# Two-layer hybrid trunk on one core: four stages of the mixer moved between attention units, and one PSUM bank left out of the rotation for a while

## The chip, the cores and the metric

The kernel runs on one core of a Trainium2 chip, in one launch, for 256 tokens of width 1024, all in float32. The metric is the device time in microseconds (us); the median of three runs before the change is 1275.85 us (1275.85 to 1276.56).

## The reference

Each of two layers does x += W_out(concat[attention(h), conv(h), retention(h)]) with h = RMSNorm(x), and then x += FFN(RMSNorm(x)): a dense SwiGLU in layer 0, a top-2-of-8 expert SwiGLU in layer 1. A last RMSNorm follows. The mixers read column groups of one projection:

```python
proj = h @ w_in
o_a = nsa_mixer(q, k_c, v_c, k_s, v_s, k_w, v_w, gl, cmp_pe, cmp_w1, cmp_w2)
o_b = conformer_conv(conv_in, conv_w, conv_b, conv_ln_g, conv_ln_b, conv_pw)
o_c = retention(rq, rk, rv, rg, ret_gn)
```

- Attention has 8 heads of 64 in 2 key groups and three branches. With 256 tokens all 4 blocks of 64 are selected and the window of 512 covers everything, so the selected branch and the window branch are both causal softmax attention, with their own keys and values. The compressed branch attends over 15 blocks; its keys and values come from `silu(flat @ w1) @ w2`, once for keys and once for values (the two "compression halves").
- Retention has 4 heads: scores q·k times a decay, then the product with v, a normalisation over each head and a gate: `o = intra + cross`, `mu`, `var`, `silu(gate) * o`.
- The convolution is depthwise with 31 taps, then a LayerNorm over channels, SiLU and a pointwise product.

## The kernel before

Every engine (TensorE, ScalarE, VectorE) walks the same static list `MIXER[l]` of stages for layer l, and takes from each stage its own part. An engine runs its parts strictly in that order; nothing overtakes. The list is the opening (`OPEN`, `HEAD`: projections, convolution taps, rotary, first scores), then 12 attention units, then `TAIL`. A unit k is a piece of one branch: 4 heads by 128 tokens or 2 heads by 128 tokens with 256 keys. Unit k is the stages

`probT k` (transpose of unit k's probabilities, copied by ScalarE), `AHEAD[k]`, `score k+2` (the scores of the unit after next: TensorE, then VectorE's row maximum, then ScalarE's exponentials), `BESIDE[k]`, `pv k` (product with the values: TensorE, then VectorE's scaling).

`BESIDE[k]` holds stages of the other mixers put into that unit. Those that the change touches:

- `rets 0`, `rets 1`: retention's scores. TensorE writes two banks each, VectorE multiplies by the decay (line 1778) into `rp0`, `rp1`.
- `convT`: TensorE transposes the convolution's output; `cnorm 0` is VectorE's mean and variance of it (lines 1805 to 1811).
- `reto`: retention's product, 12 matrix products on TensorE (each is two records in the trace, as every float32 product is), one copy by ScalarE (line 1266). It waits for all of `rets`.
- `hid 0`, `hid 1`: the first products of the two compression halves, 16 matrix products each with 32 weight columns (`128*32` in the trace), one copy by ScalarE (line 1311). They need the weights W1K and W1VN, which SyncE's queue loads.
- `retnorm 0`: VectorE's statistics of `reto` (lines 1784 to 1789); `croot`: ScalarE's inverse root for `cnorm`.

In the trace, line 661 is every matrix product and line 664 every transpose of TensorE. Line 1705 is a unit's row maximum, 1707 its negative, 1298 the exponentials, 1308 the copy of the transposed probabilities, 1712, 1716 and 1719 the scaling of `pv`. Line 1687 is VectorE's 16 additions that read the bank of `kcv` (the compressed branch's raw keys and values) into `blocks`.

PSUM has 8 banks. `GROUP` gives every stage that writes PSUM its bank, by counting round from bank 2 in the order of the list. TensorE's `begin` waits until the last user of that bank has been read (`bank_free`). The bank of a score stage is freed by ScalarE when the exponentials of that unit are done. From `out 0` on, only banks 0 to 3 rotate.

Of the kernel before, what the change touches and what calls it, by code (L numbers as in the profile page):

```python
# [76 lines left out]
def conv(a, b):  # L77
# [12 lines left out]

AHEAD = {6: [("convB", 0), ("hidT", 0), ("hidT", 1), ("rsilu", 0), ("rroot", 0)], 8: [("retcat", 0)]}

BESIDE = {0: [("rets", 0)], 1: [("rets", 1)], 2: [("convT", 0)],
          3: [("reto", 0), ("hid", 0), ("cnorm", 0)], 4: [("croot", 0), ("hid", 1), ("retnorm", 0)], 5: [("cnorm", 1)],
          6: [("retnorm", 1)], 7: [("cmpkv", 0), ("conv_pw", 0)],
          8: [("cscore", 0), ("out", 0)], 9: [("out", 1)],
          10: [("cprobT", 0), ("out", 2), ("cpv", 0), ("cpv", 1)],
# [6 lines left out]
                           for z in [("probT", k)] + AHEAD.get(k, []) + [("score", k + 2)] * (k + 2 < len(UNITS)) +  # L104
                           BESIDE[k] + [("pv", k)]] + TAIL for l in range(DEPTH)]
EARLIER = (("stat", 0), ("nT", 0), ("stat", 1), ("split", 0))
# [7 lines left out]
OUT_BANK = (4, 5, 6, 7)  # L114
FIXED = {("out", r): OUT_BANK[r] for r in range(4)}
FIXED.update({("xT", 0): 2, ("xT", 1): 3, ("xT", 2): 2, ("xT", 3): 3})
NARROW = [MIXER[l].index(("out", 0)) for l in range(DEPTH)]
BANKS = 8
# [16 lines left out]
GROUP = {}  # L135
_used = [0] * BANKS
for _l in range(DEPTH):
    _n = 2
    for _at, (_stage, _k) in enumerate(MIXER[_l]):
        for _j in range(STATED.get((_stage, _k), PSUM_GROUPS.get(_stage, 0))):  # L140
            if (_stage, _k) in FIXED:
                _b = FIXED[_stage, _k]
            else:
                _b = _n % (BANKS if _at < NARROW[_l] else OUT_BANK[0])
                _n += 1
            _used[_b] += 1
            GROUP[(_l, _stage, _k, _j)] = (_b, _used[_b])

# [2131 lines left out]
```

## Time and profile before

| | us |
|---|---|
| median of three runs | 1275.85 |
| the profiled execution's own time | 1274.48 |
| its span (first to last instruction) | 1272.5 |
| TensorE, matrix products busy in the span | 1253.3 (98%) |
| VectorE busy | 996.7 (78%) |
| ScalarE busy | 857.3 (67%) |

The span is one execution on the chip. It is 1.98 us shorter than the time of that execution, which also holds what lies around the instructions. A busy TensorE means that records of matrix products follow each other; their ends are modelled. The granted TensorE clock is 0.997 of full speed over the span. The mixer's units of layer 0 lie from 81 to 152 us, those of layer 1 from 416 to 487 us. The rest of the span is the projections, the dense FFN and the experts.

### The profile page before, as it was taken

To read this page: it belongs to the slowest core of one execution; us is meant where nothing else is said; L and a number is where in the kernel's file an instruction comes from. 1 tells how busy PE (TensorE), PEld (TensorE's weight loads), DVE (VectorE), ACT (ScalarE), POOL (GpSimd) and SP (SyncE) were. 2 spreads that over 40 slices of the span, in tenths; PEclk is the share of its full clock that TensorE was granted. 3 is DMA by queue.
4 is the path that set the end of the run, shared out by engine and by line. 5 is a ranking of instruction groups with operands and counts; after the bars stand their busy time and mean duration, and the time that the engine had idled before them with its cause. 6 is when DMAs were issued, how large, how long until landed. Compare 5 with 4: busy or idle time off the path is not lost.

```text
span 1272.5 us, 16272 instructions
## 1 busy us (share of the span) xinstructions
PE 1253.3 (98%) x6317; PEld 1015.6 (80%) x6317; DVE 996.7 (78%) x1110; ACT 857.3 (67%) x1225; POOL 31.4 (2%) x21
## 2 busy tenths in 40 slices
PE   9999999999999999999999999999999999999997
PEld 8797588888779866788888888888888888888885
DVE  4786465454569646998999989889889889889997
ACT  5435364444451544978878888878878878878885
POOL 0000000000000000010000000000000000000300
PEclk9999999999999999999999999999999999999998
DMA  9433194442521336899999999999999999999981
GB/s 366 169 143 133 67 387 174 175 190 103 198 100 71 143 132 271 335 404 373 391 371 371 389 380 375 388 369 377 396 369 379 389 374 357 396 373 353 416 368 39
DMA packets 38625, 367.62 MB, mean 289 GB/s; under 512 B 4112, under 2 KB 7312, under 8 KB 11152
## 3 DMA queue, kind: packets, MB, share of 16 engines
q1 hardware_dynamic: 35808, 356.56, 71.2%
q0 software_dynamic: 1440, 5.24, 1.1%
q10 hardware_dynamic: 1296, 4.72, 0.9%
q8 instruction: 53, 0.87, 0.3%
q14 instruction: 28, 0.23, 0.1%
HBM read 360.73 MB, written 5.77 MB: 288 GB/s over the span
## 4 chain that ended last, share of the span: by engine, by line
PE 92%; DVE 4%; ACT 2%; DMA 1%; issue 1%; SPq 0%; DVEq 0%; ACTq 0%
PE ps L661 88%; PE ps L664 3%; DMA ring<-mix_in 1%; ACT arena L1298 1%; DVE blocks L1687 1%; DVE wlU L1869 1%; DVE arena L1705 0%; DVE wlD L1876 0%; ACT arena L1308 0%; ACT L1290 0%; ACT L1345 0%; DVE arena L1778 0%; DVE xn L2112 0%; DVE hTl L1991 0%; DVE x L1833 0%
## 5 line engine op out<-in xcount | busy, mean ns | idle before, releaser
L1869 DVE TENSOR_TENSOR wlU<-ring,whU 128x2048 fp32r<-128x2048 f32 x196 | 448.9, 2290 | 57.7 <-ACT whU L1390 53.1
L1390 ACT ACTIVATE whU<-ring 128x1024 fp32r<-128x1024 f32 x396 | 417.6, 1060 | 60.8 <-PE ps L661 53.2
L661 PE MATMUL ps<-whU,hTh 128*128 128x512 f32 x880 | 352.7, 401 | 0.8 <-DVE wlU L1869 0.8
L661 PE MATMUL ps<-whU,hTl 128*128 128x512 f32 x880 | 345.0, 392 | 0.0
L661 PE MATMUL ps<-wlU,hTh 128*128 128x512 f32 x880 | 342.9, 390 | 0.0
L1876 DVE TENSOR_TENSOR wlD<-ring,whD 128x2048 fp32r<-128x2048 f32 x97 | 222.2, 2290 | 39.2 <-ACT whD L1402 39.0
L1402 ACT ACTIVATE whD<-ring 128x1024 fp32r<-128x1024 f32 x194 | 205.2, 1066 | 59.0 <-PE ps L661 52.8
L661 PEld LDWEIGHTS ps<-whU,hTl 128*128 128x128 f32 x880 | 165.1, 188 | 36.0
L661 PEld LDWEIGHTS ps<-wlU,hTh 128*128 128x128 f32 x880 | 166.1, 189 | 32.4
L661 PEld LDWEIGHTS ps<-whU,hTh 128*128 128x128 f32 x880 | 165.3, 188 | 32.7 <-DVE wlU L1869 1.0
L661 PE MATMUL ps<-whD,gTh 128*128 128x512 f32 x428 | 168.6, 394 | 0.5 <-DVE gTl L1894 0.5
L661 PE MATMUL ps<-whD,gTl 128*128 128x512 f32 x428 | 167.3, 391 | 0.0
L661 PE MATMUL ps<-wlD,gTh 128*128 128x512 f32 x428 | 166.6, 389 | 0.0
L661 PEld LDWEIGHTS ps<-whD,gTh 128*128 128x128 f32 x428 | 80.4, 188 | 19.7 <-DVE wlD L1876 3.6
L661 PEld LDWEIGHTS ps<-whD,gTl 128*128 128x128 f32 x428 | 80.3, 188 | 16.9
L661 PEld LDWEIGHTS ps<-wlD,gTh 128*128 128x128 f32 x428 | 80.7, 189 | 16.4
L1416 ACT ACTIVATE gTh<-ps 128x256 fp32r<-128x256 f32 x107 | 40.3, 386 | 54.6 <-PE ps L664 54.6
L661 PEld LDWEIGHTS ps<-arena 128*128 128x128 f32 (+1 forms) x472 | 56.6, 190 | 14.5 <-issue 12.7
L661 PE MATMUL ps<-arena 128*128 128x64 f32 (+6 forms) x472 | 65.2, 297 | 2.3 <-ACT arena L1308 2.3
L1894 DVE TENSOR_TENSOR gTl<-ps,gTh 128x256 fp32r<-128x256 f32 x107 | 44.3, 422 | 27.5 <-ACT gTh L1416 27.5
L664 PE MATMUL ps<-cst,arena 128*128 128x128 f32 x376 | 63.3, 273 | 1.2 <-DVE arena L1815 1.1
L664 PEld LDWEIGHTS ps<-cst,arena 128*128 128x128 f32 x376 | 48.2, 143 | 17.2 <-issue 3.6
(232 smaller groups left out, 1224.2 us busy)
## 6 DMA issues: line engine op xcount, KB each, us to landing
ring<-moe_in SPq DMA_DIRECT2D x88, 2048.0 KB, 8.5
ring<-moe_in SPq DMA_DIRECT2D x88, 1024.0 KB, 8.6
ring<-ffn_in SPq DMA_DIRECT2D x11, 2048.0 KB, 7.5
ring<-mix_in SPq DMA_DIRECT2D x5, 3072.0 KB, 11.0
ring<-ffn_in SPq DMA_DIRECT2D x11, 1024.0 KB, 7.2
ring<-mix_in SPq DMA_DIRECT2D x4, 2048.0 KB, 10.3
ring<-mix_in SPq DMA_DIRECT2D x2, 2176.0 KB, 8.3
ring<-mix_in SPq DMA_DIRECT2D x2, 2112.0 KB, 8.1
```

The lines of the kernel that those rows point to most:

```text
L661: return nc.tensor.matmul(o, lhsT, rhs, start=first, stop=last, skip_group_check=True)
L664: return nc.tensor.transpose(o, a, ident)
L1298: last = A(prob[:, k % 3, c * keys:(c + 1) * keys], bank(l, stage, k)[:, c * keys:(c + 1) * keys], ACT.Exp, bias=nmax[:, k, c:c + 1], scal ...
L1390: A(whU[:, p, :], ring[:, f.slot(J), p * PIECE:(p + 1) * PIECE], ACT.Copy).then_inc(s_hi, 1)
L1402: A(wh_down(f, J, c), ring[:, f.slot(J), (UP + c) * PIECE:(UP + c + 1) * PIECE], ACT.Copy)\
L1416: A(g_high(f, J, i), ps[:, up_bank(f, J, i), 0:FC].rearrange("p (c t) -> p c t", c=DOWN), ACT.Copy)\
L1687: last = V.tensor_tensor(blocks[lo:lo + HD, v, hi, :, g, 0:NBLK], src[g * HD:(g + 1) * HD, v, :, hi:hi + NBLK, r], spread(pe_[lo:lo + HD, ...
L1869: V.tensor_tensor(wlU[:, w, :], raw, whU[:, w, :].bitcast(F32), ALU.subtract).then_inc(s_lo, 1)
L1876: V.tensor_tensor(wl_down(f, J), raw, high.bitcast(F32), ALU.subtract).then_inc(s_lo, 1)
L1894: V.tensor_tensor(g_low(f, J, i), ps[:, up_bank(f, J, i), 0:FC].rearrange("p (c t) -> p c t", c=DOWN), g_high(f, J, i).bitcast(F32), ALU.s ...
```

## The change

The new order of `BESIDE` puts `rets 1` into unit 0 beside `rets 0`, `convT` into unit 1, `cnorm 0` and `reto` into unit 2, and `croot`, `hid 0` and `hid 1` into unit 3. All engines follow it. In the bank rotation, the bank of `kcv` is skipped from `kcv` until `pv 0`. All later banks of the units shift with it.

```diff
-BESIDE = {0: [("rets", 0)], 1: [("rets", 1)], 2: [("convT", 0)],
-          3: [("reto", 0), ("hid", 0), ("cnorm", 0)], 4: [("croot", 0), ("hid", 1), ("retnorm", 0)], 5: [("cnorm", 1)],
+BESIDE = {0: [("rets", 0), ("rets", 1)], 1: [("convT", 0)], 2: [("cnorm", 0), ("reto", 0)],
+          3: [("croot", 0), ("hid", 0), ("hid", 1)], 4: [("retnorm", 0)], 5: [("cnorm", 1)],
...
 for _l in range(DEPTH):
-    _n = 2
+    _n, _held = 2, None
     for _at, (_stage, _k) in enumerate(MIXER[_l]):
+        if (_stage, _k) == ("pv", 0):
+            _held = None
         for _j in range(STATED.get((_stage, _k), PSUM_GROUPS.get(_stage, 0))):
             if (_stage, _k) in FIXED:
                 _b = FIXED[_stage, _k]
             else:
-                _b = _n % (BANKS if _at < NARROW[_l] else OUT_BANK[0])
+                _wide = BANKS if _at < NARROW[_l] else OUT_BANK[0]
+                _n += _n % _wide == _held
+                _b = _n % _wide
                 _n += 1
+            if _stage == "kcv":
+                _held = _b
             _used[_b] += 1
             GROUP[(_l, _stage, _k, _j)] = (_b, _used[_b])
```

The banks of the first stages, in the order of each version (the same in both layers), with the last user of the bank behind the arrow:

```
before: kcv 3, score0 4, score1 5, probT0 6, score2 7, rets0 0 and 1, pv0 2, probT1 3<-kcv, score3 4<-score0,
        rets1 5<-score1 and 6<-probT0, pv1 7<-score2, probT2 0<-rets0
after:  kcv 3, score0 4, score1 5, probT0 6, score2 7, rets0 0 and 1, rets1 2 and 4<-score0, pv0 5<-score1,
        probT1 6<-probT0, score3 7<-score2, convT 0<-rets0, pv1 1<-rets0, probT2 2<-rets1, score4 3<-kcv
```

## Rows read from the trace of the kernel before

**Rows 1.** The page: busy time and share of each engine over the span.
```profile
PE 1253.3 (98%) x6317; PEld 1015.6 (80%) x6317; DVE 996.7 (78%) x1110; ACT 857.3 (67%) x1225; POOL 31.4 (2%) x21
```

**Rows 2.** Chain of waits that ended last, layer 0's units: start, duration, what.
```profile
88.76 1.52 ACT arena L1298 x8
...
92.65 6.50 PE ps L661 x69
...
100.73 0.70 DVE arena L1705
...
106.22 1.03 ACT arena L1298 x4
...
114.84 1.08 PE ps L661 x8
```

**Rows 3.** Timeline, TensorE's weight loads, units 0 to 4: start, duration, what, idle before.
```profile
84.00 0.97 PEld L661 LDWEIGHTS ps<-arena 128*128 128x128 f32 x8 [0.33 <-issue]
85.12 0.42 PEld L664 LDWEIGHTS ps<-cst,arena 128*128 128x128 f32 x4 [0.15 <-DVE blocks L1687]
85.51 0.10 PEld L661 LDWEIGHTS ps<-causalb,identb 128*128 128x128 bf16 x1
...
86.81 0.52 PEld L661 LDWEIGHTS ps<-arena 64*128 64x128 f32 x8
...
89.17 0.10 PEld L661 LDWEIGHTS ps<-causalb,identb 128*128 128x128 bf16 x1
...
90.04 0.57 PEld L664 LDWEIGHTS ps<-cst,arena 128*128 128x128 f32 x4
91.09 0.97 PEld L661 LDWEIGHTS ps<-arena 128*128 128x128 f32 x8 [0.48 <-issue]
91.93 0.48 PEld L664 LDWEIGHTS ps<-cst,arena 128*128 128x128 f32 x4
92.38 0.10 PEld L661 LDWEIGHTS ps<-causalb,identb 128*128 128x128 bf16 x1
...
96.17 1.45 PEld L661 LDWEIGHTS ps<-ring,blocks 128*32 128x32 f32 x32
98.04 0.97 PEld L661 LDWEIGHTS ps<-arena 128*128 128x128 f32 x8 [0.41 <-issue]
98.87 0.48 PEld L664 LDWEIGHTS ps<-cst,arena 128*128 128x128 f32 x4
99.32 0.10 PEld L661 LDWEIGHTS ps<-causalb,identb 128*128 128x128 bf16 x1
...
100.62 1.45 PEld L661 LDWEIGHTS ps<-ring,blocks 128*32 128x32 f32 x32
```

**Rows 4.** Timeline, ScalarE: end of score 2's exponentials, and the copy behind them.
```profile
86.85 0.20 ACT L1298 ACTIVATION_READ_ACCUMULATOR arena<-ps,arena 128x1 f32 x1
87.18 0.60 ACT L1308 ACTIVATE arena<-ps 128x512 f32<-128x512 f32 x1
```

**Rows 5.** Timeline, VectorE: retention's scores, and three steps behind TensorE or itself.
```profile
85.90 1.28 DVE L1778 TENSOR_TENSOR arena<-ps,cst 128x512 f32<-128x512 f32 x2
...
88.64 0.74 DVE L1778 TENSOR_TENSOR arena<-ps,cst 128x256 f32<-128x256 f32 x2
...
99.25 0.42 DVE L1719 TENSOR_TENSOR arena<-ps,arena 128x256 f32<-128x256 f32 x1 [1.25 <-PE ps L661]
...
105.31 0.68 DVE L1705 TENSOR_REDUCE arena<-ps 128x2 f32<-128x512 f32 x1
```

**Rows 6.** Timeline, layer 1's counterparts on TensorE of the rows at 85.12 and 99.32.
```profile
419.87 0.42 PEld L664 LDWEIGHTS ps<-cst,arena 128*128 128x128 f32 x4 [0.21 <-DVE blocks L1687]
...
434.08 0.10 PEld L661 LDWEIGHTS ps<-causalb,identb 128*128 128x128 bf16 x1
```

**Rows 7.** Table by stretch: busy time and count of each engine, clock, DMA share, GB/s.
```profile
92.65:99.60 6.95, 6.95 (x74) 5.84 (x74) 4.45 (x11) 2.60 (x7) 0.00 (x0) 1.00 0.17 68
...
95.00:96.00 1.00, 1.00 (x12) 1.00 (x10) 0.93 (x3) 0.61 (x4) 0.00 (x0) 1.00 0.00 0
...
114.84:140.00 25.16, 25.16 (x132) 16.16 (x133) 11.15 (x38) 8.69 (x26) 0.00 (x0) 1.00 0.37 155
```

## The prediction

> **What bounds the kernel now.** I read the page's busy shares first, then the chain of waits, then the timeline of each engine between 81 and 115 us, where the changed stages lie.
>
> TensorE is busy for 98% of the span [rows 1], so most of the kernel can't be touched by this change. What can be touched is the stretch in which the chain leaves TensorE: in layer 0 it passes over ScalarE's exponentials of score 3 at 88.76, returns to TensorE, which it holds without a break from 92.65 to past 99, goes to VectorE at 100.73 (the maximum of score 6), to ScalarE at 106.22 (exponentials of score 7) and comes back to TensorE for good at 114.84 (pv 7) [rows 2]. In the stretch 92.65 to 99.60 TensorE's busy time is 6.95 of 6.95 us, while VectorE has 4.45 and ScalarE 2.60; from 114.84 to 140.00 TensorE is busy for 25.16 of 25.16 [rows 7]. So whatever delays score 7's exponentials at 106.22 delays pv 7 at 114.84 and all that follows, and nothing later in the layer gives it back: the order behind it is the same and TensorE has no gap there.
>
> Layer 1 repeats this: its probT 1 starts at 419.87 and its score 6 at 434.08, 334.75 and 334.76 us after those of layer 0 (85.12, 99.32) [rows 3, 6]. Hence one layer is worked out and the result doubled.
>
> What each of TensorE's stages takes is read from start to start of its weight loads [rows 3]: pv 0.84 (91.09 to 91.93); probT 0.45 (91.93 to 92.38), and the same for convT, which is also four transposes; a score with 256 keys 0.87 (89.17 to 90.04); score 3 1.19 (85.51 to 86.81 is 1.30, of which I leave 0.11 for the change to another row form behind it); hid 1.87 (96.17 to 98.04); reto 2.92 (score 5 starts at 92.38, plus 0.87 is 93.25, and hid 0 starts at 96.17).
>
> **The change, part by part.**
>
> *The bank of kcv.* Before, probT 1 takes kcv's bank and starts at 85.12, released by VectorE's additions of line 1687 [rows 3]. That wait goes: probT 1 now takes probT 0's bank. But the shifted rotation puts score 3 into score 2's bank, which ScalarE frees only after the exponentials of unit 2. Their last step ends at 87.05 (86.85 + 0.20) and ScalarE's next copy starts at 87.18 [rows 4]; I take 87.18 as the moment at which score 3 starts, with 87.05 and 87.4 as ends. Before, score 3 started at 85.51 [rows 3]. So what is late next is score 3, by 1.67. What TensorE had to do in the meantime (rets 1, pv 0, probT 1) is done before: pv 0 started at 84.00, rets 1's loads take 0.52, so pv 0 goes to 84.52 and probT 1 to 85.36 and ends at 85.81 [rows 3]. TensorE then stands still for 87.18 - 85.81 = 1.37. Other new neighbours in the rotation were read by then or are waited for anyway (probT k needs the exponentials of unit k, so score k+2 in score k's bank costs nothing; only score 3 on score 2 is one unit too early).
>
> *rets 1 into unit 0.* On TensorE it falls into that idle time and costs nothing; if the bank didn't hold score 3, it would cost its 0.52. On VectorE it stands now before pv 0 and before score 3's maximum: its two instructions take 0.74 busy [rows 5]. The maximum would come 0.7 later, about when score 3 is there anyway (87.18 plus 1.41, the distance from score 6's start at 99.32 to its maximum at 100.73 [rows 2, 3]). The exponentials of score 3 go from 88.76 to about 89.5; they take 1.52 [rows 2], and the copy of probT 2 behind them 0.60, so it ends at 91.6 or, with the handovers, 91.8. pv 2, which waits for it, will be later than that (below), so this delay of 0.75 has 2 us of cover.
>
> *convT into unit 1.* It moves ahead of pv 1, and score 4 no longer has it behind it: 0.45 of TensorE at another place, in the sum below.
>
> *cnorm 0 and reto into unit 2.* reto's 2.92 on TensorE moves from behind score 5 to before pv 2. Before, TensorE was idle there for 0.48 at 91.09 [rows 3], so at most that much is won from hiding. VectorE's cnorm 0 now stands between score 4's maximum and pv 2, under reto as it stood under reto and hid 0 before; VectorE waits for TensorE at 99.25 for 1.25 [rows 5] and will again. I cost it at nothing; without the cover of reto it would hold back pv 2's scaling, but nothing on TensorE.
>
> *hid 1 into unit 3.* This is the dear part. Before, hid 1 started at 100.62, behind score 6 [rows 3], and TensorE ran it while VectorE did score 6's maximum, retnorm 0, pv 4 and reached score 7 at 105.31 without waiting for TensorE [rows 5]: it was free. Now it stands in front of pv 3, probT 4 and score 6, on the path. Its price is 1.87, less what two hid in a row save. The first hid's 32 weight loads end at 97.62 and the next load comes at 98.04, after 0.41 of idle [rows 3]. The matrix products of a hid are 32 with 1.87 from start to start; four column groups run side by side, so I take 1.70 for the first of a pair (0.17 of run-out saved) and 1.87 for the second, 3.57 together. The bounds are 3.74 (nothing saved) and 3.33 (the whole 0.41 saved).
>
> The Trainium skill ("TensorEngine Tiling (Array Packing)", Key Properties) says that changing the tiling mode drains TensorE, while tiles of one mode run in parallel. The gap of 0.41 behind hid 0 agrees [rows 3]. If all of the gap is that drain, putting hid 1 behind hid 0 saves it whole and the sum below would be 0.24 smaller in each layer, 2.6 us in all, an estimate.
>
> *What the weights need.* hid 1 will start at 97.8 instead of 100.62. The DMA share is 0.00 from 95 to 96 [rows 7]: the weights are there. The later loads hang on cmpkv in unit 7 and move with everything.
>
> **The sum.** From the start of score 3 to that of score 6 TensorE now does score 3 1.19, convT 0.45, pv 1 0.84, probT 2 0.45, score 4 0.87, reto 2.92, pv 2 0.84, probT 3 0.45, score 5 0.87, the two hid 3.57, pv 3 0.84, probT 4 0.45: 13.74. No step in it waits for another engine: pv 1 comes at 88.8 (its copy starts at 87.18 and takes 0.60 [rows 4]), pv 2 at 93.9 against a copy that ends at 91.8. So score 6 starts at 87.18 + 13.74 = 100.92 instead of 99.32, 1.60 later. I round the row form changes, of which one is gone with reto no longer before hid, to 0.05 less: 1.55 in a layer. From there VectorE's line (score 6, retnorm 0, pv 4, score 7) and ScalarE's (its exponentials, the table load, to pv 7) are as long as before. Two layers: 3.1 us. The profiled execution would take 1274.48 + 3.1 = 1277.6, and its span 1275.6; the median of the runs shown is 1.37 above the profiled one, and so 1275.85 + 3.1 = 1279.0. Ends of the unknowns: release of score 3 at 87.05 or 87.4, the pair at 3.33 or 3.74, give 1.2 to 2.0 in a layer, so 1278.2 to 1279.8.
>
> **The rivals.**
>
> *The bank doesn't hold score 3* (the wait for score 2's exponentials is over earlier than I read, or TensorE has other things to do). Then score 3 starts at 85.81, pv 1 waits for its copy (87.18 + 0.60 [rows 4]) until about 87.8, and from there 13.74 - 1.19 - 0.45 = 12.10 remain to score 6: 99.9, 0.6 late, 1275.85 + 1.2 = 1277.05. For it: TensorE's records show no wait that is marked for a bank of exponentials. Against: the release at 87.05 comes from the written order. This is "no change" as a measurement goes.
>
> *reto hides* (the faster side). Place: unit 2, between score 4 and pv 2. If TensorE, delayed by the bank, has a stand there as long as reto, because the exponentials of score 3 and the copy of probT 2 come late as well, then reto's 2.92 leaves the path of unit 3 and only hid 1 enters it: 1.55 - 2.92 = -1.37 in a layer, 1275.85 - 2.7 = 1273.1. It decides from the point at which TensorE needs no more than 99.32 - 87.18 = 12.14 from score 3 to score 6. For it: the busy records have modelled ends, and only 0.48 of idle is marked before pv 2, which may be short of the truth. Against: VectorE has to wait 1.25 for TensorE at 99.25 [rows 5], and reto's loads run at the spacing of a busy engine.
>
> *More waits than read.* VectorE's late score 3 (0.75) reaches the path after all, or hid 1 finds its weights late: 1.55 + 0.75 = 2.3 in a layer, 1280.45. Against: 2 us of cover, and the idle DMA at 95.
>
> **How the numbers follow.** About 0.2% (2.55 us) is what a measurement of this kernel can tell from no change. The forecast has 0.55, the free bank 0.15, the hidden reto 0.17, more waits 0.10, and 0.03 is for anything else. Of the forecast's own range 1278.2 to 1279.8 the part above 1278.4 counts as slower, about 0.42 of the 0.55; with more waits 0.52, rounded to 0.53. Faster is 0.17 and a little of the rest, 0.18. The remainder, 0.29, is no change. The range takes in the forecast, the free bank, the more likely part of the reto case and most of the case with more waits: 1273.0 to 1280.4. The forecast's own is 1278.2 to 1279.8.
>
> **What would show it.** Right: in the trace after, TensorE stands still for about 1.4 us before score 3 and starts it when ScalarE's exponentials of unit 2 end; from score 3 to score 6 it needs 13.7 without an idle stretch; the two blocks of 32 loads of 128*32 lie next to each other, some 1.7 apart; score 6's maximum comes 1.5 later relative to the end of kcv's additions, and the distance from it to pv 7 (100.73 to 114.84 [rows 2], 14.11) is unchanged. Wrong: score 3 starts before the exponentials of unit 2 end; TensorE idles before pv 2 or between pv 3 and score 6; VectorE arrives at score 7 after waiting for TensorE; or the distance to pv 7 shrinks, which would mean that hid 1 had been on the path there.

## The result, and the profile after

| | before | changed |
|---|---|---|
| median of seven runs | 1275.8 us (1274.64 to 1276.56) | 1280.55 us (1279.52 to 1282.27) |
| ratio of the runs, 95% interval | | 1.0042 (1.0032 to 1.0052) |
| profiled execution: time, span, granted clock | 1274.48, 1272.5, 0.997 | 1281.63, 1279.6, 0.993 |

The changed kernel is slower by 4.75 us. 3.1 had been forecast, with a range up to 1280.4, so the time lies just outside; a second set of runs (below, 1279.86) lies inside. In the two profiled executions the spans are 7.1 apart.

The walk from kcv's additions to score 6 came out as worked out, as a whole. Timeline of TensorE's weight loads in the changed kernel, layer 0 (start, duration, engine, what; in brackets the idle time before):

```profile
85.21 0.48 PEld L670 LDWEIGHTS ps<-cst,arena 128*128 128x128 f32 x4
87.07 0.10 PEld L667 LDWEIGHTS ps<-causalb,identb 128*128 128x128 bf16 x1 [1.38 <-ACTq L1309]
...
89.80 0.10 PEld L667 LDWEIGHTS ps<-causalb,identb 128*128 128x128 bf16 x1
...
94.74 0.10 PEld L667 LDWEIGHTS ps<-causalb,identb 128*128 128x128 bf16 x1
...
95.91 3.18 PEld L667 LDWEIGHTS ps<-ring,blocks 128*32 128x32 f32 x64 [0.33 <-issue]
99.50 0.97 PEld L667 LDWEIGHTS ps<-arena 128*128 128x128 f32 x8 [0.41 <-issue]
...
100.78 0.10 PEld L667 LDWEIGHTS ps<-causalb,identb 128*128 128x128 bf16 x1
...
105.52 0.97 PEld L667 LDWEIGHTS ps<-arena 128*128 128x128 f32 x8 [1.51 <-issue]
...
108.36 0.72 PEld L670 LDWEIGHTS ps<-cst,arena 128*128 128x128 f32 x4 [1.53 <-issue]
109.06 1.83 PEld L667 LDWEIGHTS ps<-fold,arena 128*128 128x128 f32 x8
```

The first of kcv's additions starts at 81.49 here against 81.58 before, so times of the two traces are compared after adding 0.09. Score 3 stands still for 1.38 behind a step of ScalarE's queue (line 1309, which frees the bank of score 2) and starts at 87.07. Score 6 starts at 100.78, 13.71 later, against 99.32 before [rows 3]: 1.55 late. The length of 13.71 (13.74 foreseen, less 0.05) holds some luck: score 3 takes 1.01 here, not 1.19, and score 4, reto and pv 2 take 4.49 together, not 4.63, while score 5 takes 1.17, not 0.87, since a gap of 0.33 now stands between it and hid 0. The misses cancel. The 64 loads at 95.91 are hid 0 and hid 1. The last rows answer to [rows 3] too, and they are the ones I had not asked about: TensorE now stands still for 1.51 before pv 5 and for 1.53 before convB. In their place the kernel before has idle times of 0.24 and 0.74. After them the same eight loads against `fold` (hidT) take 1.83, where they take 0.97 in the kernel before. The same view of the kernel before:

```profile
104.84 0.97 PEld L661 LDWEIGHTS ps<-arena 128*128 128x128 f32 x8 [0.24 <-issue]
...
106.89 0.42 PEld L664 LDWEIGHTS ps<-cst,arena 128*128 128x128 f32 x4 [0.74 <-issue]
107.28 0.97 PEld L661 LDWEIGHTS ps<-fold,arena 128*128 128x128 f32 x8
```

The longer loads come from the clock. Table by stretch of the changed kernel (busy time and count of PE, PEld, DVE, ACT and POOL, then granted clock, DMA share, GB/s):

```profile
104.00:106.00 2.00, 0.87 (x6) 0.49 (x6) 1.93 (x3) 1.24 (x5) 0.00 (x0) 1.00 0.00 0
106.00:108.00 2.00, 1.07 (x10) 0.83 (x9) 1.86 (x8) 0.31 (x1) 0.00 (x0) 0.93 0.00 0
108.00:110.00 2.00, 1.61 (x9) 1.64 (x9) 0.77 (x4) 1.81 (x6) 0.00 (x0) 0.50 0.00 0
110.00:112.00 2.00, 2.00 (x9) 1.82 (x10) 0.00 (x0) 1.99 (x5) 0.00 (x0) 0.50 0.00 0
112.00:114.00 2.00, 2.00 (x10) 1.82 (x8) 0.98 (x3) 1.98 (x3) 0.00 (x0) 0.50 0.00 0
...
500.00:502.00 2.00, 2.00 (x12) 2.00 (x13) 0.33 (x1) 0.19 (x1) 0.00 (x0) 0.56 1.09 459
```

and the same stretches of the kernel before:

```profile
106.00:108.00 2.00, 1.47 (x15) 1.26 (x13) 1.29 (x5) 1.61 (x5) 0.00 (x0) 1.00 0.00 0
108.00:110.00 2.00, 2.00 (x17) 1.90 (x17) 0.62 (x1) 1.97 (x4) 0.00 (x0) 1.00 0.00 0
```

TensorE is busy for 0.87 and 1.07 of 2 us in two neighbouring stretches, and from 108 to 114 it runs at 0.50 of full speed: the lower of its two levels, 1.2 instead of 2.4 GHz. What TensorE does then (convB, hidT, score 8) gets onto the path; VectorE waits for it. Timeline of VectorE, changed kernel:

```profile
112.99 0.69 DVE L1711 TENSOR_REDUCE arena<-ps 128x2 f32<-128x512 f32 x1 [4.14 <-PE ps L667]
```

In the kernel before this maximum of score 8 starts at 109.38 (timeline of VectorE, kernel before):

```profile
109.38 0.69 DVE L1705 TENSOR_REDUCE arena<-ps 128x2 f32<-128x512 f32 x1 [2.00 <-PE ps L661]
```

The clock also falls at 500, at the router of layer 1.

A ruler for all traces below: the distance from the first of kcv's additions to the 53 products that begin with score 10. In the chain of waits (start, duration, what) of the changed kernel, layer 0 and layer 1:

```profile
81.49 0.84 DVE blocks L1693 x4
...
120.50 7.33 PE ps L667 x53
...
420.07 0.84 DVE blocks L1693 x4
...
456.84 7.33 PE ps L667 x53
```

and in that of the kernel before:

```profile
81.58 0.84 DVE blocks L1687 x4
...
116.80 7.34 PE ps L661 x53
...
416.33 0.84 DVE blocks L1687 x4
...
451.56 7.33 PE ps L661 x53
```

That is 39.01 and 36.77, where the kernel before has 35.22 and 35.23 (116.80 - 81.58 and 451.56 - 416.33). Layer 1, without a fall of the clock, costs 1.54: the order alone. Layer 0 costs 3.79, that is 1.55 for the order and 2.24 for the clock. From the router's products to the first `pick` product it is 9.54 (507.78 - 498.24) instead of 7.84 (500.80 - 492.96), 1.70 for the clock. Timeline of TensorE, changed kernel, then kernel before:

```profile
498.24 5.00 PE L667 MATMUL ps<-router,hTr 128*128 128x8 f32 x32
...
507.78 2.15 PE L667 MATMUL ps<-pick,xh 128*128 128x256 f32 x16
```
```profile
492.96 3.64 PE L661 MATMUL ps<-router,hTr 128*128 128x8 f32 x32
...
500.80 2.17 PE L661 MATMUL ps<-pick,xh 128*128 128x256 f32 x16 [0.72 <-DVE pick L1972]
```

Layer 0, layer 1 and router together: 1.54 + 3.79 + 1.70 = 7.03 of the 7.1 between the spans.

The 1.70 at the router need not be the change's. The profiled execution of the kernel before, 1274.48, is shorter than all seven runs of the table. In a later set of 18 runs of that kernel, the four with a mean granted clock of 0.995 took 1275.85 to 1276.52 us, the nine with 0.997 or more 1274.3 to 1275.34. It loses time to the clock in some executions too; at which place, those runs don't tell. So the medians, 4.75 apart, say more of the change than these two spans.

### The profile page after: what moved, and what is told of

The parts are those of the page before. It is cut to its first block, busy times and chain, and to the rows that moved or that the text cites. A ratio compares the mean times of both kernels' runs of the same rounds, so it can differ in the third digit from the quotient of the medians.

```text
span 1279.6 us, 16272 instructions
## 1 busy us (share of the span) xinstructions
PE 1257.0 (98%) x6317; PEld 1020.1 (80%) x6317; DVE 996.8 (78%) x1110; ACT 857.7 (67%) x1225; POOL 31.0 (2%) x21
## 4 chain that ended last, share of the span: by engine, by line
PE 93%; DVE 4%; ACT 1%; DMA 1%; issue 0%; SPq 0%; DVEq 0%; ACTq 0%
PE ps L667 90%; PE ps L670 4%; DMA ring<-mix_in 1%; DVE blocks L1693 1%; DVE wlU L1875 1%; DVE wlD L1882 0%; ACT arena L1304 0%; DVE arena L1711 0%; DVE xn L2118 0%; DVE hTl L1997 0%; DVE x L1839 0%; ACT xn L1202 0%; DVE arena L1792 0%; DVE arena L1793 0%; DVE arena L1794 0%
```

## The experiments

"Changed" is the kernel with the change; each diff is against it unless said otherwise. The rulers of all kernels stand in a table at the end. Where an expectation counts 33.3 us from the end of kcv's additions to pv 7, this is the way from the start of the first of them (114.84 - 81.58 = 33.26 [rows 2]).

**hid 1 back in unit 4**

```diff
-          3: [("croot", 0), ("hid", 0), ("hid", 1)], 4: [("retnorm", 0)], 5: [("cnorm", 1)],
+          3: [("croot", 0), ("hid", 0)], 4: [("hid", 1), ("retnorm", 0)], 5: [("cnorm", 1)],
```

> The changed kernel, but with hid 1 back in unit 4, behind score 6. Theory (hid 1 on TensorE's path, and the slow clock only a follow-up of the idle time that it left behind in unit 4): score 6 starts 1.70 earlier than in the changed kernel, at about 99.1, from the end of kcv's additions to pv 7 it takes what it took before within 0.2 us (33.3), the granted clock stays at 1.00 in units 5 and 6, and the time is 1275.5 us, ratio to before 0.9997 (0.999 to 1.0005). Rival (the bank of score 2 or the earlier reto costs the time): the time stays at 1279 or more.

Measured: 1274.89 us against 1275.26, ratio 0.9998 (0.9989 to 1.0007). Chain of this kernel, and TensorE's loads (start, duration, what):

```profile
81.28 0.84 DVE blocks L1693 x4
...
116.33 7.33 PE ps L667 x53
```
```profile
86.85 0.10 PEld L667 LDWEIGHTS ps<-causalb,identb 128*128 128x128 bf16 x1 [1.39 <-ACTq L1309]
...
98.84 0.10 PEld L667 LDWEIGHTS ps<-causalb,identb 128*128 128x128 bf16 x1
100.15 1.45 PEld L667 LDWEIGHTS ps<-ring,blocks 128*32 128x32 f32 x32
...
104.37 0.97 PEld L667 LDWEIGHTS ps<-arena 128*128 128x128 f32 x8 [0.23 <-issue]
...
106.42 0.42 PEld L670 LDWEIGHTS ps<-cst,arena 128*128 128x128 f32 x4 [0.74 <-issue]
```

The stand of 1.39 before score 3 is still there, and so are rets 1, convT and reto in their new units; the loss is gone. The ruler is 35.05, and the idle times before pv 5 and convB are back to 0.23 and 0.74. The clock stays at 1.00 in the units. So all of the loss hangs on hid 1's place.

**Only hid 1 moved** (against the kernel before)

```diff
-          3: [("reto", 0), ("hid", 0), ("cnorm", 0)], 4: [("croot", 0), ("hid", 1), ("retnorm", 0)], 5: [("cnorm", 1)],
+          3: [("reto", 0), ("hid", 0), ("hid", 1), ("cnorm", 0)], 4: [("croot", 0), ("retnorm", 0)], 5: [("cnorm", 1)],
```

> The kernel before, with one thing moved: hid 1 from unit 4 to unit 3, directly behind hid 0; nothing else of the change, the old bank rule. Theory: 1.7 us in each layer on TensorE before score 6, and idle TensorE in units 4 and 5, so the clock falls as in the changed kernel: 3.4 for the order and 0 to 4 for the clock, 1279.2 to 1283, middle 1280.5, ratio 1.0027 to 1.0055. Rival (hid 1 harmless, the rest costs): 1275.8, ratio 1.000.

Measured: 1280.32 us, ratio 1.0047 (1.0033 to 1.0061). The rulers are 36.96 (81.45 to 118.41) and 39.31 (417.96 to 457.27). The order costs 1.74; in the changed kernel a second hid adds 1.72 to the first (3.59 - 1.87). TensorE stands still for 1.77 and 1.26 in layer 0 before pv 5 and convB, for 2.06 and 0.98 in layer 1, and the clock fell this time in layer 1, for 2.35 more (table by stretch, columns as above):

```profile
444.00:446.00 2.00, 1.23 (x8) 1.02 (x7) 1.40 (x6) 1.48 (x5) 0.00 (x0) 0.65 0.00 0
446.00:448.00 2.00, 2.00 (x11) 2.00 (x11) 0.00 (x0) 1.97 (x4) 0.00 (x0) 0.50 0.03 8
```

hid 1 alone makes the whole loss. The rest of the change (the bank, rets 1, convT, cnorm, reto) is worth 1.74 - 1.55 = 0.19 in a layer, close to the 0.17 that the first experiment won.

**TensorE kept busy where it stands still**

```diff
 elif stage == "pv":
     o = begin(l, stage, k)
+    if k == 5:
+        keep_busy(o, 10)
...
 elif stage == "convB":
     o = begin(l, stage)
+    keep_busy(o, 10)
```

> The changed kernel, with ten extra matrix products of the zero tile (256 columns, bf16, about 1.07 us together) in front of pv 5's wait and ten in front of convB's wait, where TensorE stands still; their result is overwritten. Theory (the clock fell because TensorE stood still twice for 1.5 us): the granted clock stays 1.00 from 106 to 116, layer 0 from the end of kcv's additions to pv 7 takes 33.3 + 1.55 = 34.8 instead of 37.0, and the time falls by about 2.2 to 1278.3; if the fall of the clock at the router is a follow-up as well, by 3.9 to 1276.6. Rival (the clock falls whatever TensorE does there, or the slow stretch in units 5 and 6 is a wait of another kind): layer 0 keeps its 37 us and the time is 1280.5 or more.

Measured: 1278.68 us, ratio 1.0026 (1.0016 to 1.0037). Rulers 36.78 and 36.77, the clock at 1.00 in the units of both layers. Loads of TensorE in this kernel:

```profile
103.74 1.19 PEld L667 LDWEIGHTS ps<-warm 128*128 128x128 bf16 x10
105.16 0.97 PEld L667 LDWEIGHTS ps<-arena 128*128 128x128 f32 x8 [0.23 <-ACT arena L1317]
...
106.44 1.08 PEld L667 LDWEIGHTS ps<-warm 128*128 128x128 bf16 x10
108.01 0.42 PEld L670 LDWEIGHTS ps<-cst,arena 128*128 128x128 f32 x4 [0.48 <-DVE arena L1824]
108.39 0.97 PEld L667 LDWEIGHTS ps<-fold,arena 128*128 128x128 f32 x8
```

Twenty products more in a layer, and the kernel is no slower but faster: its mean is 3.4 us above that of the kernel before in its own set of runs, where the changed kernel's was 5.1 above and, run again, 4.8. The intervals of the ratios still overlap (1.0037 against 1.0032 and 1.0025), so the firmer sign is the trace: `fold` takes 0.97 again. What stays is the order's loss. The fall at the router stayed in this trace (9.15 from products to `pick`).

**Banks of score 3 and score 4 exchanged**

```diff
+SWAP = {("score", 3): 3, ("score", 4): 7}
...
                 _n += 1
+                _b = SWAP.get((_stage, _k), _b)
```

> The changed kernel with the banks of score 3 and score 4 exchanged: score 3 takes kcv's bank, score 4 that of score 2. Theory (score 3 waits 1.4 us for the bank of score 2): score 3 starts at 85.65 instead of 87.07, pv 1 is then held by its copy until 87.85 instead of starting at 88.52, so everything from pv 1 to score 6 is 0.67 earlier in each layer, 1.3 together: 1279.2 with the clock as before, ratio 1.0027. Rival (TensorE's stand before score 3 is not a bank wait): score 3 stays at 87.07 and the time at 1280.5.

Measured: 1280.24 us, ratio 1.0042 (1.0028 to 1.0055): in time not told apart from the changed kernel. The loads show that score 3 did wait for the bank all the same:

```profile
85.10 0.10 PEld L669 LDWEIGHTS ps<-causalb,identb 128*128 128x128 bf16 x1
...
99.53 0.10 PEld L669 LDWEIGHTS ps<-causalb,identb 128*128 128x128 bf16 x1
...
104.27 0.97 PEld L669 LDWEIGHTS ps<-arena 128*128 128x128 f32 x8 [1.50 <-issue]
```

From the additions (80.96) to score 6 it is 18.57 instead of 19.29, 0.72 less. But both stands are still there, and the clock fell in both layers: rulers 36.98 and 38.52, where 36.77 - 0.72 = 36.05 would be the order's. In this trace the clock cost 0.93 + 2.47, more than in either trace of the changed kernel at the units, and so a gain of 1.4 us in the two layers doesn't show in the time.

**The two kernels once more**

> The changed kernel once more, unchanged, for a second trace. Theory: both layers take 1.55 more than before for the order (score 6 starts 19.3 after the first of kcv's additions), and where the slow clock falls differs from run to run: in layer 0's units 5 and 6, in layer 1's, or at the router, each worth up to 2.3 us; time 1280.5, ratio 1.0042. Rival (the place of the slow clock is fixed by the order of the instructions): again exactly layer 0's units 5 and 6 and the router.

Measured: 1279.86 us, ratio 1.0039 (1.0025 to 1.0053). Rulers 37.70 and 37.70: this time the clock fell in both layers for a shorter stretch (0.93 each), and the fall at the router cost nothing (7.85). Same instructions, other places: the order of the stages doesn't fix in which layer the clock falls.

> The kernel before once more, for a second trace. Theory: the granted clock stays at 1.00 in the units of both layers (no stand of 1.5 us there); at the router, where TensorE does products of 8 columns and waits, it may fall, for up to 1.7 us. Rival (the slow clock comes with any run): a fall in the units too.

Measured: 1274.37 us, in one run. Rulers 35.22 and 35.23, clock 1.00 in all units. At the router it fell to 0.50 from 498 to 500 and cost nothing (7.85), since it hit the filling products in front of a wait (14 of them take 2.49 there instead of 1.69, and the idle 0.77 behind them is gone).

**Both repairs** (hid 1 in unit 4, and the banks exchanged: both diffs above)

> The changed kernel with both repairs: hid 1 back in unit 4, and the banks of score 3 and score 4 exchanged. Theory (both parts add): hid 1 alone gave -0.17 a layer against before, the banks gave 0.72 a layer on the way to score 6, so score 6 starts 0.9 earlier than before in each layer and the time is 1275.3 - 1.8 = 1273.5, ratio 0.9986 (0.9975 to 0.9995), clock at 1.00 in the units. Rival (the earlier score 6 only meets the next wait): 1275, ratio 1.000.

Measured: 1272.7 us, ratio 0.9979 (0.9969 to 0.9989), rulers 34.33 and 34.32, clock 1.00 in the units: 0.9 less than before in each layer, as expected. The parts add; the time is 0.8 below the expected 1273.5, inside its range of ratios.

**hid 1 and retnorm 0 in unit 5** (with the banks exchanged)

```diff
-          3: [("croot", 0), ("hid", 0), ("hid", 1)], 4: [("retnorm", 0)], 5: [("cnorm", 1)],
+          3: [("croot", 0), ("hid", 0)], 4: [], 5: [("hid", 1), ("cnorm", 1), ("retnorm", 0)],
```

> As the one with both repairs, but hid 1 and retnorm 0 both in unit 5 (in the order hid 1, cnorm 1, retnorm 0), so that neither TensorE's hid 1 nor VectorE's 3.2 us of retnorm 0 stands between score 6 and score 7. Theory (from score 6 on the path leads over retnorm 0, pv 4 and score 7's maximum): the exponentials of score 7 come some 3 earlier than before, the copy of probT 6 then waits for TensorE's hid 1 and comes 2.1 earlier, and the time is 1275.3 - 4.2 = 1271.1, ratio 0.9967 (0.996 to 0.998). Rival (ScalarE's or TensorE's other work in units 5 and 6 takes the place of the wait): no more than with both repairs, 1273.5.

Measured: 1271.38 us, ratio 0.9965 (0.9951 to 0.9978), the fastest kernel of the study. Rulers 33.31 (81.66 to 114.97) and 33.31, 1.9 less than before in each layer. Timeline of ScalarE in this kernel:

```profile
103.11 0.47 ACT L1306 ACTIVATE arena<-ps,arena 128x256 f32<-128x256 f32 x1
...
105.59 0.60 ACT L1316 ACTIVATE arena<-ps 128x512 f32<-128x512 f32 x1 [0.95 <-PE ps L672]
```

The exponentials of score 7 start 21.45 after kcv's additions (103.11 - 81.66) instead of 24.64 (106.22 - 81.58 [rows 2]), 3.2 earlier, and then, as expected, the copy of probT 6 waits 0.95 for TensorE; it starts 1.9 earlier than before (2.1 expected). The kernel's span, 1270.5, still holds a fall of the clock at the router (8.66).

**One stand filled at a time** (the two additions of the third experiment, each alone)

> The changed kernel with ten extra matrix products of the zero tile in front of pv 5's wait only; the stand before convB stays 1.5 us. Theory (it takes both stands close together to lose the clock; the kernel before had one of 0.74 and none of 1.5): the clock stays at 1.00 in the units of both layers, each layer 36.8 from kcv's additions to score 10, time 1278.7. Rival (one stand of 1.5 is enough): the clock falls in one or both layers and the time is 1279.5 to 1281.

Measured: 1279.8 us, ratio 1.0038 (1.0024 to 1.0052). Rulers 36.78 and 39.36. The theory that it takes both stands is wrong: with pv 5's filled, the one before convB, 1.60 long, sufficed in layer 1 and did not in layer 0:

```profile
444.02 0.51 PEld L670 LDWEIGHTS ps<-cst,arena 128*128 128x128 f32 x4 [1.60 <-issue]
444.51 1.83 PEld L667 LDWEIGHTS ps<-fold,arena 128*128 128x128 f32 x8
```

> The changed kernel with ten extra matrix products of the zero tile in front of convB's wait only; the stand before pv 5 stays 1.5 us. Theory and rival as for the first stand: clock at 1.00 in both layers, 36.8 each and 1278.7; or a fall in one or both and 1279.5 to 1281.

Measured: 1278.21 us, ratio 1.0027 (1.0016 to 1.0037), rulers 36.76 and 36.76, clock 1.00 in both layers although the stand of 1.50 before pv 5 is there. In this trace the stand before convB is the one that counts. The mean granted clock of all runs says that this is no accident of one trace: it lies at 0.995 to 0.998 in all nine runs here and at 0.995 to 0.997 in the eight with both stands filled, as in the kernel before (0.995 to 0.999 in 44 runs); it lies at 0.994 to 0.995 in the five with only pv 5's filled, at 0.992 to 0.994 in the changed kernel's seven runs and at 0.992 to 0.996 in its five later ones. The mean times over the kernel before in the same set of runs go the same way: 3.4 here, 4.8 with only pv 5's stand filled.

The rulers (us) and the way at the router, from one trace each; 35.2 and 7.84 are the undisturbed values of before:

| kernel | layer 0 | layer 1 | router |
|---|---|---|---|
| before; again | 35.22; 35.22 | 35.23; 35.23 | 7.84; 7.85 |
| changed; again | 39.01; 37.70 | 36.77; 37.70 | 9.54; 7.85 |
| hid 1 back in unit 4 | 35.05 | 35.04 | 8.10 |
| only hid 1 moved | 36.96 | 39.31 | 7.85 |
| both stands filled | 36.78 | 36.77 | 9.15 |
| banks exchanged | 36.98 | 38.52 | 7.84 |
| both repairs | 34.33 | 34.32 | 9.29 |
| hid 1, retnorm 0 in unit 5 | 33.31 | 33.31 | 8.66 |
| first stand filled | 36.78 | 39.36 | 7.85 |
| second stand filled | 36.76 | 36.76 | 7.85 |

## Why the prediction was right in most steps and wrong in its sum

- *The bank.* Right. Score 3 was foreseen at 87.18 and came at 87.07 + 0.09 = 87.16, after a stand of 1.38 (1.37 foreseen). The exchange of banks showed that it is a bank wait, worth 0.72 in a layer. The rival in which the bank does not hold score 3 fell with it.
- *rets 1, convT, cnorm 0.* Right: no cost on the path. The kernel with hid 1 put back holds all of them and is not slower.
- *reto.* Right: it fills TensorE before pv 2. The rival in which it hides for the gain of 2.92 failed; what the whole rest of the change gives is 0.17 in a layer.
- *hid 1.* Right in mechanism and size: two hid in a row take 99.50 - 95.91 = 3.59 (3.57 foreseen), score 6 is 1.55 late (1.55), the latter by terms whose misses cancel (see above). The row form change that the sum called gone is not: a gap of 0.33 stands before the pair. The whole 0.41 of the gap behind a hid is not saved: the pair takes 0.15 less than twice 1.87, so the estimate made from the Trainium skill's rule on tiling ("TensorEngine Tiling (Array Packing)", Key Properties), 2.6 us in all, did not hold.
- *The step that failed*, in the prediction's words: "From there VectorE's line (score 6, retnorm 0, pv 4, score 7) and ScalarE's (its exponentials, the table load, to pv 7) are as long as before." VectorE's part is: score 7's maximum comes 4.57 after score 6's, 106.77 - 102.20, against 105.31 - 100.73 = 4.58 [rows 2, 5]. From score 6's maximum to pv 7 it was 14.11 [rows 2], and it is 14.11 again in layer 1 of the first trace (454.88 - 440.77), where the clock did not fall. In layer 0 it is 16.21 (118.41 - 102.20): ScalarE's copy for pv 7 is over at 116.16, and TensorE comes 2.2 after it, since it did convB to probT 7 at the low clock. So the line to pv 7 is longer than before when the clock falls, and the prediction put that at nothing. I costed hid 1 only where it arrives. Where it left, TensorE's idle time before pv 5 and convB grew from 0.24 and 0.74 to 1.51 and 1.53, and the clock fell at or behind these stands, for 2.24 in the one trace and 1.86 in the other. That is the missing term of the sum: the order's 3.1 came out (3.08 in the rulers), and the other 1.65 of the 4.75 between the medians is what the clock leaves to explain, more in the profiled execution, less in others.

The rows behind the last point: TensorE's loads for pv 7 in layer 0, and the chain of waits in layer 1, both of the changed kernel.

```profile
118.41 1.07 PEld L667 LDWEIGHTS ps<-arena 128*128 128x128 f32 x8
```
```profile
440.77 0.70 DVE arena L1711
...
454.88 1.08 PE ps L667 x8
```

Filling the stand before convB took the loss of the clock in the units away and left that of the order; putting hid 1 back took away both. Counted over all traces, two layers each: with the stands left open (the changed kernel twice, only hid 1 moved, banks exchanged) the clock fell in 6 of 8 layers; with only pv 5's filled in 1 of 2; with convB's filled in 0 of 4; with hid 1 in unit 4 or 5 in 0 of 10.

What stays open is which amount of standing makes the clock fall in a given layer, and why the router's fall costs between 0 and 1.7 us. The router's fall is in eleven of the twelve traces, also in those of the kernels that are faster than the one before (1.45 and 0.82 there), so it does not hang on hid 1; whether the change makes it dearer on average isn't shown. In the kernel before it was there in one trace out of two, and cost nothing.

## What to carry to other kernels

Work moved off an engine's idle time can cost twice: once where it lands on the path, and once where it leaves a hole. Before moving TensorE work out of a stage that waits for VectorE and ScalarE, add up how long TensorE will stand there, and look at the granted clock of the stretch behind it. With a static rotation of buffers, walk the new order once and compare each owner's release with its successor's start; one exchanged pair gave 0.72 us in each layer here. When one trace of a kernel shows a slow stretch, measure stage distances in a second one before giving it to a wait.

## What the runs showed of the hardware

- The granted clock fell from 1.00 to 0.50 after a single stand of 1.60 us in one layer (0.97 to 1.83 for the same eight loads) and not after the same stand in the other layer of the same execution (only pv 5's stand filled). With idle times of 0.24 and 0.74 at these places it did not fall in the units in any of four traces (the kernel before twice, hid 1 back in unit 4, both repairs).
- The Trainium skill ("TensorE: Matmul & The Clock Gate", Part 1) describes the two levels, 1.2 and 2.4 GHz, and calls the moment at which the higher one is granted at a kernel's start variable from run to run. The 0.50 of full speed in these traces is the lower level, and the moment varies here too, though for a fall in mid-kernel: two executions of the changed kernel lost 2.24 and 0, and 0.93 and 0.93, in their two layers.
- Ten products of a zero tile in front of a wait (1.08 us) cost nothing on the path (rulers 36.76 with them before convB, 36.77 in a layer of the changed kernel without a fall) and made the kernel faster: its mean is 3.4 us above that of the kernel before in the same set of runs, against 5.1 and 4.8 without them.
